# First stage of a two-block fp32 kernel: x's norm by pairs of tiles while x lands, the condition's weights by pairs, and the first four fills interleaved

## The chip, the core and the metric

The kernel runs on one NeuronCore of a Trainium2 chip. The metric is the device time of one execution in microseconds; lower is better. The core has five engines that run their own instruction streams and meet only at semaphores: TensorE (PE, matrix products), VectorE (DVE), ScalarE (ACT), GpSimd (POOL) and SyncE (SP), which here only issues DMAs.

## What is computed

The reference is two transformer-like blocks over x (512 positions by 1,024 channels), all in float32. The change touches only the first lines of the first block:

```python
cond = jax.nn.silu(c.astype(jnp.float32))
mod = cond @ w_ada[l] + b_ada[l]
sh1, sc1, g1, sh2, sc2, g2 = [m[:, None, :] for m in jnp.split(mod, 6, axis=-1)]
u = _layer_norm(h) * (1.0 + sc1) + sh1          # h = x
z = u @ w_in[l]                                 # then HGRN2, gMLP, gates, projections
...
h = _layer_norm(DEEPNORM_ALPHA * h + g1 * mix) * ln1_w[l] + ln1_b[l]
u2 = _layer_norm(h) * (1.0 + sc2) + sh2         # then the FFN, and a second block
```

`_layer_norm` subtracts the mean over the 1,024 channels and divides by the root of the variance. c is one vector of 1,024, w_ada is 1,024 by 6,144.

## The kernel before

x lies transposed in SBUF as `H`: eight tiles (`DT`) of 128 channels by `T` = 512 positions. `bank(b)` is one of the eight PSUM banks, 128 by 512 floats; `A(kb, n, at)` is a stretch of the work area `arena`, and `C("ones", n)` a matrix of ones, so that a product with it sums over the partitions and leaves the sum in every row.

**Fills.** A weight matrix comes in fills: a fill holds the weights of 128 output channels for all eight input tiles (512 KB). SP loads fill n into place n mod 2 of `w_raw`; ScalarE rounds it to fp32r as `w_hi` (`first_hi` L1215, later `hi`), place n mod 4; POOL subtracts and leaves the rest as `w_lo` (`lo_part` L370, four instructions, semaphore `lo_ready`). The same is done to the normed input: `XH` is rounded by ScalarE (`first_x` L1236), `XL` is the remainder from VectorE (`low` L1764). `blocks` (L405) then issues three products of 128x128 by 128x512 for each input tile, `w_hi` with `XH`, `w_lo` with `XH` and `w_hi` with `XL`: 24 products a fill. The last of a fill raises `fill_done`. Only then may ScalarE take the output (`take_hgrn` L1254) and write fill n+4 into the same place of `w_hi`; SP may load over a place of `w_raw` when the fill in it has been split (`lo_ready`).

**The first stage in order.** SP issues x by pairs of tiles (four DMAs), fills 0 and 1, the four parts of w_ada's first 2,048 columns (16 KB a partition each; parts 0 and 1 hold the shift `sh1`, 2 and 3 the scale `sc1`), and then a fill whenever `lo_ready` allows; before fill 4 it also waits for `ada_done` to be 4 and issues four later chunks of w_ada. TensorE sums x (L553, eight products), waits for the squares and sums them (`squares_sum` L524, eight), and in between multiplies the condition with w_ada (`condition_rows` L562: eight products into 32 rows each, four column groups of the array) and turns the result into columns (`condition_columns` L569, four products of one column). Between them stand `idle_products` (L495), products of ones that nobody reads. VectorE centres x (`centred` L1753), multiplies by the root (L1895), adds the bias to the modulation (L1898), and from parts 2 and 3 on scales and shifts tile by tile (L1906). ScalarE squares (L1181), copies the rows out of PSUM (`rows_out` L1229) and computes the root as exp(-0.5 ln v) (`rstd` L1142, L1144). Then fills 0 and 1 go tile by tile in turn, as the tiles become ready, and fills 2 and 3 whole:

```python
first_two(0, 0, 0, lambda t: pe.wait_ge(sem("ln_x"), t + 1))
next_two(0, 0, 0)
gemm(4, 1, 20)
```

After 24 fills TensorE waits for `ada_done` to be 36: VectorE has by then multiplied the later chunks of w_ada with the condition (L1918, L1921). From there on the program is the same in both kernels but for the numbers that semaphores are waited for.

## Time and profile before

| | |
|---|---|
| median of 3 runs | 2936.79 us (2935.02 to 2938.13) |
| the profiled execution's own time | 2937.75 us |
| its span in the profile | 2936.0 us |
| TensorE busy | 2904.3 us, 99% |
| VectorE, ScalarE, POOL busy | 1295.5, 1112.1, 1476.9 us |
| mean granted TensorE clock | 0.998 of full speed |

The page says at a glance which engine has no room: TensorE. Averages say little about the first 63 us, which are 2% of the span, so that stage is read from the timeline (one engine, in order of time), from windows and from the landing times of DMAs. A product's busy time runs over into the next one's (ends are modelled), so the distance of two starts is what one costs.

### The profile page before, as it was taken

The page shows a single profiled execution, that of the slowest core. Times are in us where ns is not written, and L with a number is a line of the kernel's source. Part 1 is how long each engine was busy: PE and PEld are TensorE (multiplying, and loading weights), DVE is VectorE, ACT ScalarE, POOL GpSimd, SP SyncE. Part 2 cuts the span into 40 slices and gives each one's busy share as a digit, 9 for nine tenths or more (in the row PEclk, how much of TensorE's full clock was granted, in tenths as well). Part 3 has the DMA queues.
Part 4 walks back from the last instruction along what each step waited for, and adds up shares of the span by engine and source line. Part 5 has one row for each costly group of instructions (what it writes and reads, how often), then busy time and mean ns, then how long its engine had stood idle before and what let it go on. Part 6 is the DMA issues. An engine that isn't in the chain of part 4 may idle for free.

```text
span 2936.0 us, 52696 instructions
## 1 busy us (share of the span) xinstructions
PE 2904.3 (99%) x20922; PEld 2333.3 (79%) x20922; DVE 1295.5 (44%) x1818; ACT 1112.1 (38%) x1610; POOL 1476.9 (50%) x1824
## 2 busy tenths in 40 slices
PE   9999999999999999999999999999999999999999
PEld 5887778778888777777778888887777777888887
DVE  5837742381110658443757222225944375722210
ACT  4445653243222443225554322224322556432222
POOL 4543345545555556224337555665623343755555
PEclk9999999999999999999999999999999999999999
DMA  6731122213323233225343323333322633423233
GB/s 264 280 103 51 51 94 93 93 58 101 99 96 104 79 122 119 74 79 209 115 158 117 99 93 100 100 107 105 132 71 78 217 111 136 141 94 99 93 102 127
DMA packets 104764, 335.25 MB, mean 114 GB/s; under 512 B 10608, under 2 KB 11024, under 8 KB 103824
## 3 DMA queue, kind: packets, MB, share of 16 engines
q1 hardware_dynamic: 77648, 277.06, 28.5%
q10 hardware_dynamic: 26944, 55.67, 5.1%
q8 instruction: 135, 2.21, 0.3%
q14 instruction: 37, 0.30, 0.0%
HBM read 303.84 MB, written 28.84 MB: 113 GB/s over the span
## 4 chain that ended last, share of the span: by engine, by line
issue 45%; POOL 39%; PE 14%; DVE 1%; POOLq 1%; DMA 0%; ACT 0%; DVEq 0%; SPq 0%; ACTq 0%
POOL w_lo L376 39%; PE psum L405 14%; PE psum L553 0%; POOLq L372 0%; DVE HL L1743 0%; POOLq L382 0%; DVE arena L1753 0%; DVE arena L2379 0%; DMA w_raw<-in_fills 0%; DVEq L1740 0%; PE psum L495 0%; ACT w_hi L1110 0%; DMA par<-in_par 0%; ACT arena L1181 0%; ACT w_hi L1217 0%
## 5 line engine op out<-in xcount | busy, mean ns | idle before, releaser
L376 POOL TENSOR_TENSOR w_lo<-w_raw,w_hi 128x256 fp32r<-128x256 f32 x1820 | 1476.7, 843 | 1454.3 <-ACT w_hi L1110 1306.1
L405 PE MATMUL psum<-XH,w_hi 128*128 128x512 f32 x2592 | 1043.9, 403 | 10.7 <-DVE arena L1989 3.5
L405 PE MATMUL psum<-XL,w_hi 128*128 128x512 f32 x2592 | 1012.3, 391 | 0.0
L405 PE MATMUL psum<-XH,w_lo 128*128 128x512 f32 x2592 | 1012.1, 390 | 0.0
L1110 ACT ACTIVATE w_hi<-w_raw 128x1024 fp32r<-128x1024 f32 x436 | 460.3, 1056 | 689.8 <-PE psum L405 565.0
L405 PEld LDWEIGHTS psum<-XH,w_hi 128*128 128x128 f32 x2592 | 487.3, 188 | 137.0 <-issue 21.1
L405 PEld LDWEIGHTS psum<-XL,w_hi 128*128 128x128 f32 x2592 | 487.6, 188 | 104.3
L405 PEld LDWEIGHTS psum<-XH,w_lo 128*128 128x128 f32 x2592 | 488.1, 188 | 98.5 <-issue 4.8
L405 PE MATMUL psum<-HH,w_hi 128*128 128x512 f32 x976 | 382.0, 391 | 2.5 <-DVE HL L1743 1.5
L405 PE MATMUL psum<-HL,w_hi 128*128 128x512 f32 x976 | 379.9, 389 | 0.0
L405 PE MATMUL psum<-HH,w_lo 128*128 128x512 f32 x976 | 379.8, 389 | 0.0
L405 PEld LDWEIGHTS psum<-HH,w_hi 128*128 128x128 f32 x976 | 183.3, 188 | 42.9 <-DVE HL L1743 3.0
L405 PEld LDWEIGHTS psum<-HL,w_hi 128*128 128x128 f32 x976 | 183.2, 188 | 38.4
L405 PEld LDWEIGHTS psum<-HH,w_lo 128*128 128x128 f32 x976 | 183.3, 188 | 37.4 <-issue 0.2
L805 PEld LDWEIGHTS psum<-arena 64*64 64x64 f32 x6848 | 132.2, 134 | 41.5 <-issue 31.7
L805 PE MATMUL psum<-arena 64*64 64x64 f32 (+1 forms) x6848 | 147.0, 223 | 2.4 <-ACT arena L1580 1.5
L1743 DVE TENSOR_TENSOR HL<-arena,HH 128x512 f32 (+2 forms) x114 | 96.9, 859 | 111.1 <-ACT HH L1212 40.6
L1212 ACT ACTIVATE HH<-arena 128x512 f32 x44 | 27.9, 633 | 189.5 <-DVE arena L1852 189.5
L1535 ACT ACTIVATE arena<-psum 128x512 f32<-128x512 f32 x88 | 52.2, 593 | 107.7 <-PE psum L405 107.3
L1847 DVE TENSOR_TENSOR arena<-psum,arena 128x512 f32<-128x512 f32 x44 | 30.4, 692 | 140.1 <-PE psum L405 120.6
L1776 DVE TENSOR_TENSOR arena<-psum,arena 128x512 f32<-128x512 f32 x22 | 15.2, 691 | 171.9 <-PE psum L405 171.9
L1852 DVE TENSOR_TENSOR arena<-psum,arena 128x512 f32<-128x512 f32 x44 | 30.4, 692 | 116.0 <-PE psum L405 115.4
(341 smaller groups left out, 2368.3 us busy)
## 6 DMA issues: line engine op xcount, KB each, us to landing
w_raw<-in_fills SPq DMA_DIRECT2D x456, 512.0 KB, 3.4
scratch<-arena ACTq DMA_DIRECT2D x86, 256.0 KB, 2.1
arena<-in_fills SPq DMA_DIRECT2D x32, 512.0 KB, 4.5
arena<-scratch ACTq DMA_DIRECT2D x10, 1024.0 KB, 7.5
arena<-in_w_ada SPq DMA_DIRECT2D x4, 2048.0 KB, 19.0
H<-scratch ACTq DMA_DIRECT2D x4, 2048.0 KB, 11.4
scratch<-H SPq DMA_DIRECT2D x2, 2048.0 KB, 8.0
arena<-scratch SPq DMA_DIRECT2D x32, 128.0 KB, 3.8
```

The lines of the kernel that those rows point to most:

```text
L376: ins = nc.gpsimd.tensor_tensor(w_lo[:, to:to + FILL // 4], w_raw[:, of:of + FILL // 4], w_hi[:, to:to + FILL // 4].bitcast(F32), ALU.subt ...
L405: ins = mm(out_ap, wt[:, w:w + 128], xt[:, x0:x0 + T], start=first and k == 0 and o == 0, stop=last and k == n - 1 and o == 2)
L805: ins = mm(bank(b, n, at)[to:to + 64], left[r], right[r], start=first, stop=last)
L1110: fn(w_hi[:, s * FILL:(s + 1) * FILL], w_raw[:, (s % 2) * FILL:(s % 2 + 1) * FILL], ACT.Copy).then_inc(hi_ready, 1)
L1212: fn(HH[:, bass.ds((2 * i + j // 2) * T, T)], A(105, T, j // 2 * T), ACT.Copy).then_inc(sem("ffn_hi"), 1)
L1535: fn(buffer, bank(b), ACT.Sigmoid if GATE_B <= k < RG_AT else ACT.Copy).then_inc(chunk_out[b], 1)
L1743: return tt(dst, src, hi_part.bitcast(F32), ALU.subtract)
L1776: tt(A(105, T, k * T), bank(j), A(88, T, k * T), ALU.mult).then_inc(chunk_out[j], 1)
L1847: tt(A(88, T, k * T), bank(j - 1), A(R_KB), ALU.mult).then_inc(chunk_out[j - 1], 1)
L1852: tt(A(105, T, k * T), bank(j), A(88, T, k * T), ALU.mult).then_inc(chunk_out[j], 1)
```

## The change

- SP: w_ada comes in four pieces by pairs of tiles: piece k holds the shift and the scale of tiles 2k and 2k+1, in two DMAs of 8 KB a partition. The order is x, piece 0, fills 0 and 1, piece 1; then a wait for `lo_ready` 1, fill 2, piece 2; a wait for `lo_ready` 2, fill 3, piece 3. The later chunks of w_ada stand before fill 6 instead of fill 4.
- Norm: the first two tiles of x give a shift (their mean over 256 channels). VectorE adds it to each pair as it has landed, ScalarE squares, and TensorE sums both by pairs into column groups of 32; a total over the groups gives mean and variance. ScalarE squares the mean.
- VectorE subtracts the mean in place (L1962), multiplies by scale and root at once (`scaled`), ScalarE adds the shift as the activation's bias while rounding, and VectorE adds it again for the remainder (`first_low`).
- TensorE: the first four fills go by pairs of tiles, with the condition's products among them; the idle groups of products from L495 behind the second go.

```diff
@@ -285,10 +287,25 @@
             for q in range(4):
                 part = slice(2 * q * T, (2 * q + 2) * T)
                 sp.dma_start(H[:, part], dram["x"][:, part]).then_inc(x_in[q], 16)
+            def ada_piece(k):
+
+                for half in range(2):
+                    of = dram["w_ada"][2 * half + k // 2][:, k % 2 * 8 * KB:(k % 2 + 1) * 8 * KB]
+                    sp.dma_start(A(40 + 16 * k + 8 * half, 8 * KB), of).then_inc(sem(f"ada_in{k}"), 16)
+
+            def first_fill(f):
+
+                sp.dma_start(w_raw[:, f % 2 * FILL:(f % 2 + 1) * FILL], dram["fills"][f]).then_inc(w_loaded[f % 2], 16)
+
+            ada_piece(0)
             for f in range(2):
-                sp.dma_start(w_raw[:, f * FILL:(f + 1) * FILL], dram["fills"][f]).then_inc(w_loaded[f], 16)
-            for k in range(4):
-                sp.dma_start(A(40 + 16 * k, 16 * KB), dram["w_ada"][k]).then_inc(sem(f"ada_in{k}"), 16)
+                first_fill(f)
+            ada_piece(1)
+            for f in range(2, 4):
+                sp.wait_ge(lo_ready, f - 1)
+                first_fill(f)
+                ada_piece(f)
+
...
-            for n in range(2, FILLS_HG + 4 * HEADS // 2 + 2):
+            for n in range(4, FILLS_HG + 4 * HEADS // 2 + 2):
                 a = 2 * (n - 6 - ADA_FILL) + 4
-                if n == 4:
+                if n == 6:
                     sp.wait_ge(sem("ada_done"), 4)
                     for k in range(4):
                         ada_chunk(k)
-            def squares_sum(n):
-
-                for t in range(DT):
-                    if t % 2 == 0:
-                        pe.wait_ge(sem("ln_sq"), 4 * n + t // 2 + 1)
-                    ins = mm(bank(5), C("ones", 128), A(16, T, t * T), start=t == 0, stop=t == DT - 1)
-                ins.then_inc(sem("ln_var"), 1)
+            def group_pair(b, q, tile):
+
+                for t in (2 * q, 2 * q + 1):
+                    g = 32 * (t % 4)
+                    ins = mm(bank(b)[g:g + 32], C("ones", 32), tile(t), start=t < 4, stop=t >= 4)
+                return ins
+
+            def total(b, n):
+
+                pe.wait_ge(sem("ln_groups"), n)
+                return mm(bank(b), C("ones", 128), A(GROUPS_KB), start=True, stop=True)
...
             idle_products(3, 3)
-            for t in range(DT):
-                if t % 2 == 0:
-                    pe.wait_ge(x_in[t // 2], 16)
-                ins = mm(bank(4), C("ones", 128), H[:, t * T:(t + 1) * T], start=t == 0, stop=t == DT - 1)
+            pe.wait_ge(x_in[0], 16)
+            for t in range(2):
+                ins = mm(bank(0), C("ones", 128), H[:, t * T:(t + 1) * T], start=t == 0, stop=t == 1)
             ins.then_inc(sem("ln_sum"), 1)
+            idle_products(2, 3)
+
+            def shifted_pair(q):
+
+                pe.wait_ge(sem("ln_xc"), q + 1)
+                return group_pair(1, q, lambda t: A(0, T, t * T))
+
+            def squared_pair(q):
+
+                pe.wait_ge(sem("ln_sq"), q + 1)
+                return group_pair(3, q, lambda t: A(16, T, t * T))
+
+            shifted_pair(0)
+            for q in range(1, 4):
+                ins = shifted_pair(q)
+                if q == 3:
+                    ins.then_inc(sem("ln_sum"), 1)
+                squared_pair(q - 1)
+            squared_pair(3).then_inc(sem("ln_sum"), 1)
+            total(2, 1).then_inc(sem("ln_sum"), 1)
 
             def condition_rows(k):
 
-                pe.wait_ge(sem(f"ada_in{k}"), 16)
+                pe.wait_ge(sem(f"ada_in{k}"), 32)
                 w = A(40 + 16 * k, 16 * KB).rearrange("p (t k c) -> p t k c", k=DT, c=128)
...
                 for t in range(4):
-                    ins = mm(bank(k, 1, t), A(ROW_KB, 128, k % 2 * T + 128 * t), C("ones", 1), start=True, stop=True)
+                    ins = mm(bank(4 + k % 2, 1, t), A(ROW_KB, 128, k % 2 * T + 128 * t), C("ones", 1), start=True, stop=True)
                 ins.then_inc(sem("ada_used"), 1)
 
             pe.wait_ge(sem("cond"), 2)
-            idle_products(2, 3)
             condition_rows(0)
-            squares_sum(0)
+            total(0, 2).then_inc(sem("ln_var"), 1)
+            condition_columns(0)
             condition_rows(1)
-            condition_columns(0)
+
+            def first_part(f, k):
+
+                if k == 0:
+                    pe.wait_ge(lo_ready, f + 1)
+                pe.wait_ge(sem("ln_x"), k + 1)
+                ins = blocks(f, XH, XL, bank(f), [k], [k], k == 0, k == DT - 1)
+                if k == DT - 1:
+                    ins.then_inc(fill_done, 1)
+
+            def first_pair(f, q):
+
+                for k in (2 * q, 2 * q + 1):
+                    first_part(f, k)
+
+            first_pair(0, 0)
+            condition_columns(1)
+            first_pair(1, 0)
             condition_rows(2)
-            condition_columns(1)
-            idle_products(2, 4)
+            first_pair(0, 1)
+            first_pair(1, 1)
+            condition_columns(2)
+            for q in range(3):
+                first_pair(2, q)
+            first_pair(0, 2)
+            first_pair(1, 2)
             condition_rows(3)
-            condition_columns(2)
-            idle_products(1, 4)
+            first_pair(3, 0)
+            first_pair(3, 1)
             condition_columns(3)
-            idle_products(3, 4)
-            first_two(0, 0, 0, lambda t: pe.wait_ge(sem("ln_x"), t + 1))
-            next_two(0, 0, 0)
+            first_pair(3, 2)
+            for f in range(4):
+                first_pair(f, 3)
             gemm(4, 1, 20)
             pe.wait_ge(sem("ada_done"), 4 + ADA_LATER)
...
+            act.wait_ge(sem("ln_sum"), 4)
+            fn(A(FIRST_SQ_KB), bank(2), ACT.Square, scale=1.0 / 32 / D).then_inc(sem("ln_sq"), 1)
             rows_out(0)
-            for f in range(2):
-                first_hi(f)
-            ln_rstd(0, RSTD_KB)
+            first_hi(0)
+            ln_rstd(0, RSTD_KB, 0, 1.0 / 32 / D)
+            first_hi(1)
 
             def first_x(t):
 
                 act.wait_ge(sem("ln_u"), t + 1)
-                fn(XH[:, t * T:(t + 1) * T], A(16, T, t * T), ACT.Copy).then_inc(sem("ln_hi"), 1)
-
-            for k in range(1, 4):
-                rows_out(k)
-            for t in range(DT):
-                first_x(t)
-                if t == 1:
-                    first_hi(2)
-            first_hi(3)
+                fn(XH[:, t * T:(t + 1) * T], A(16, T, t * T), ACT.Identity, bias=mod[:, t:t + 1]).then_inc(sem("ln_hi"), 1)
+
+            for k in range(4):
+                if k:
+                    rows_out(k)
+                    if k < 3:
+                        first_hi(1 + k)
+                for t in (2 * k, 2 * k + 1):
+                    first_x(t)
...
-            def centred(n, mean):
-
-                dve.wait_ge(sem("ln_sum"), mean)
-                for q in range(4):
-                    stt(chunks(A(0, 2 * T, 2 * q * T), T), bc(bank(4), 2), -1.0 / D, chunks(Ht(2 * q, 2), T), ALU.mult, ALU.add)\
-                        .then_inc(sem("ln_xc"), 1)
-            centred(0, 1)
-            dve.wait_ge(sem("ln_rstd"), 1)
+            dve.wait_ge(sem("ln_sum"), 1)
+            ts(A(FIRST_SHIFT_KB), bank(0), -1.0 / (2 * P), None, ALU.mult)
+            drain()
             for q in range(4):
+                dve.wait_ge(x_in[q], 16)
+                tt(chunks(A(0, 2 * T, 2 * q * T), T), chunks(Ht(2 * q, 2), T), bc(A(FIRST_SHIFT_KB), 2), ALU.add).then_inc(sem("ln_xc"), 1)
+            dve.wait_ge(sem("ln_sum"), 2)
+            cp(A(GROUPS_KB), bank(1)).then_inc(sem("ln_groups"), 1)
+            dve.wait_ge(sem("ln_sq"), 5)
+            stt(A(GROUPS_KB), A(FIRST_SQ_KB), -D / 4.0, bank(3), ALU.mult, ALU.add).then_inc(sem("ln_groups"), 1)
+
+            def centred(q):
+
                 x = chunks(A(0, 2 * T, 2 * q * T), T)
-                tt(x, x, bc(A(RSTD_KB), 2), ALU.mult)
+                stt(x, bc(bank(2), 2), -1.0 / 32 / D, x, ALU.mult, ALU.add)
+
+            def shift_scale(ap):
+
+                return ap.rearrange("p (a n) -> p a n", a=2)
+
+            def modulation(k):
+
+                dve.wait_ge(sem("ada_used"), k + 2)
+                tt(shift_scale(mod[:, 0:16])[:, :, 2 * k:2 * k + 2], shift_scale(bank(4 + k % 2, 4)),
+                   shift_scale(P1("b_ada", 0, 16))[:, :, 2 * k:2 * k + 2], ALU.add)
+                drain()
+                ts(mod[:, 8 + 2 * k:10 + 2 * k], mod[:, 8 + 2 * k:10 + 2 * k], 1.0, None, ALU.add)
+                drain()
+
+            def scaled(t):
+
+                stt(A(16, T, t * T), A(0, T, t * T), mod[:, 8 + t:9 + t], A(RSTD_KB), ALU.mult, ALU.mult).then_inc(sem("ln_u"), 1)
+
+            def first_low(t):
+
+                dve.wait_ge(sem("ln_hi"), t + 1)
+                s = slice(t * T, (t + 1) * T)
+                stt(XL[:, s], A(16, T, t * T), mod[:, t:t + 1], XH[:, s].bitcast(F32), ALU.add, ALU.subtract).then_inc(sem("ln_x"), 1)
+
+            centred(0)
+            centred(1)
             for k in range(4):
-                dve.wait_ge(sem("ada_used"), k + 2)
-                tt(mod[:, 4 * k:4 * k + 4], bank(k, 4), P1("b_ada", 4 * k, 4), ALU.add)
+                modulation(k)
+                if k == 0:
+                    dve.wait_ge(sem("ln_rstd"), 1)
+                for t in (2 * k, 2 * k + 1):
+                    scaled(t)
                 if k < 2:
-                    continue
-                drain()
-                ts(mod[:, 4 * k:4 * k + 4], mod[:, 4 * k:4 * k + 4], 1.0, None, ALU.add)
-                drain()
-                t0 = 4 * (k - 2)
-                for t in range(t0, t0 + 4):
-                    ts(A(16, T, t * T), A(0, T, t * T), mod[:, 8 + t:9 + t], mod[:, t:t + 1], ALU.mult, ALU.add).then_inc(sem("ln_u"), 1)
-                    if t > t0:
-                        low(0, t - 1)
-                low(0, t0 + 3)
```

How the orders of three engines change. SP, at the start of the program (`in_w_ada` are the condition's weights), before:

```order
L287 DMA H<-in_x 128x1024 x4
L289 DMA w_raw<-in_fills 128x1024 x2
L291 DMA arena<-in_w_ada 128x4096 x4
L315 DMA w_raw<-in_fills 128x1024 [waits lo_ready] x2
L299 DMA arena<-in_fills 128x1024 [waits ada_done]
L299 DMA arena<-in_fills 128x1024 x3
L315 DMA w_raw<-in_fills 128x1024 [waits lo_ready] x6
```

and now:

```order
L289 DMA H<-in_x 128x1024 x4
L294 DMA arena<-in_w_ada 128x2048 x2
L298 DMA w_raw<-in_fills 128x1024 x2
L294 DMA arena<-in_w_ada 128x2048 x2
L298 DMA w_raw<-in_fills 128x1024 [waits lo_ready]
L294 DMA arena<-in_w_ada 128x2048 x2
L298 DMA w_raw<-in_fills 128x1024 [waits lo_ready]
L294 DMA arena<-in_w_ada 128x2048 x2
L332 DMA w_raw<-in_fills 128x1024 [waits lo_ready] x2
L316 DMA arena<-in_fills 128x1024 [waits ada_done]
```

Pieces 2 and 3 of the condition's weights now stand behind a wait for the split of fills 0 and 1.

TensorE, from the second wait for the condition's weights on (L562 and L602 are rows, L569 and L609 columns), before:

```order
L562 MATMUL psum<-arena 32x512 [waits ada_in1]
L562 MATMUL psum<-arena 32x512 x7
L569 MATMUL psum<-con,arena 128x1 [waits ada_row]
L569 MATMUL psum<-con,arena 128x1 x3
L562 MATMUL psum<-arena 32x512 [waits ada_in2]
```

and now, to the first product of the second fill's first pair:

```order
L602 MATMUL psum<-arena 32x512 [waits ada_in1]
L602 MATMUL psum<-arena 32x512 x7
L422 MATMUL psum<-XH,w_hi 128x512 [waits ln_x,lo_ready]
L422 MATMUL psum<-XH,w_lo 128x512
L422 MATMUL psum<-XL,w_hi 128x512
L422 MATMUL psum<-XH,w_hi 128x512 [waits ln_x]
L422 MATMUL psum<-XH,w_lo 128x512
L422 MATMUL psum<-XL,w_hi 128x512
L609 MATMUL psum<-con,arena 128x1 [waits ada_row]
L609 MATMUL psum<-con,arena 128x1 x3
L422 MATMUL psum<-XH,w_hi 128x512 [waits ln_x,lo_ready]
```

The first products of fill 0 come between the rows of piece 1 and their columns; before, all rows and columns came first.

ScalarE, from the first copy of rows on, before:

```order
L1229 ACTIVATE arena<-psum 128x512 [waits ada_done]
L1217 ACTIVATE w_hi<-w_raw 128x1024 [waits w_loaded0]
L1217 ACTIVATE w_hi<-w_raw 128x1024 [waits w_loaded1]
L1142 ACTIVATE arena<-psum,con 128x512 [waits ln_var]
L1144 ACTIVATE arena<-arena 128x512
L1229 ACTIVATE arena<-psum 128x512 [waits ada_done] x3
```

and now:

```order
L1294 ACTIVATE arena<-psum 128x512 [waits ln_sum]
L1291 ACTIVATE arena<-psum 128x512 [waits ada_done]
L1279 ACTIVATE w_hi<-w_raw 128x1024 [waits w_loaded0]
L1204 ACTIVATE arena<-psum,con 128x512 [waits ln_var]
L1206 ACTIVATE arena<-arena 128x512
L1279 ACTIVATE w_hi<-w_raw 128x1024 [waits w_loaded1]
L1303 ACTIVATE XH<-arena,mod 128x512 [waits ln_u] x2
L1291 ACTIVATE arena<-psum 128x512 [waits ada_done]
L1279 ACTIVATE w_hi<-w_raw 128x1024 [waits w_loaded0]
```

Fill 1 is split behind the root, and the split of fill 0 stands behind the squared mean.

## Rows read from the trace of the kernel before

**Rows 1.** The page, section 1: busy us, share of the span and instructions of each engine.

```profile
PE 2904.3 (99%) x20922; PEld 2333.3 (79%) x20922; DVE 1295.5 (44%) x1818; ACT 1112.1 (38%) x1610; POOL 1476.9 (50%) x1824
```

**Rows 2.** Windows: length, busy us of each engine, clock, DMA share, GB/s.

```profile
0.00:40.00 40.00, 34.40 (x154) 17.38 (x155) 14.54 (x33) 15.98 (x20) 5.74 (x12) 1.00 0.87 345
...
62.70:171.50 108.80, 108.80 (x482) 89.98 (x480) 73.47 (x115) 44.91 (x50) 67.99 (x84) 1.00 0.66 237
```

**Rows 3.** Timeline, TensorE: start us, us, engine, line, op, count, [idle before <-releaser].

```profile
6.91 8.76 PE L553 MATMUL psum<-H,con 128*128 128x512 f32 x16
...
10.36 0.19 PEld L553 LDWEIGHTS psum<-H,con 128*128 128x128 f32 x1 [0.42 <-issue]
...
17.94 1.92 PE L562 MATMUL psum<-arena 128*32 128x512 f32 x16 [1.40 <-DMA arena<-in_w_ada]
...
28.71 1.05 PE L569 MATMUL psum<-con,arena 128*128 128x1 f32 x8
...
34.01 1.92 PE L562 MATMUL psum<-arena 128*32 128x512 f32 x16 [0.44 <-DMA arena<-in_w_ada]
...
39.63 0.47 PE L405 MATMUL psum<-XH,w_hi 128*128 128x512 f32 x1
...
46.31 0.50 PE L405 MATMUL psum<-XH,w_hi 128*128 128x512 f32 x1 [0.75 <-DVE XL L1743]
...
62.78 0.39 PE L405 MATMUL psum<-XH,w_hi 128*128 128x512 f32 x1
```

**Rows 4.** DMAs: the condition's issue, its landings, and the page's fills.

```profile
5.47 1.99 SPq L291 DMA_DIRECT2D arena<-in_w_ada  x4
...
DMA to landing us min/median/max: 12.4/19.0/27.0
...
w_raw<-in_fills SPq DMA_DIRECT2D x456, 512.0 KB, 3.4
```

**Rows 5.** Timeline, VectorE, columns as in rows 3.

```profile
15.71 4.62 DVE L1753 SCALAR_TENSOR_TENSOR arena<-psum,H 128x1024 f32<-128x1024 f32 x4 [7.69 <-PE psum L553]
...
38.68 0.69 DVE L1743 TENSOR_TENSOR XL<-arena,XH 128x512 fp32r<-128x512 f32 x1 [0.24 <-ACT XH L1239]
...
41.24 2.38 DVE L1743 TENSOR_TENSOR XL<-arena,XH 128x512 fp32r<-128x512 f32 x2
...
43.76 0.47 DVE L1902 TENSOR_SCALAR mod<-mod 128x4 f32<-128x4 f32 x1
...
151.01 5.17 DVE L1921 SCALAR_TENSOR_TENSOR arena<-arena,cond 128x256 f32<-128x256 f32 x7
```

**Rows 6.** Timeline, ScalarE, columns as in rows 3.

```profile
16.97 4.45 ACT L1181 ACTIVATE arena<-arena 128x1024 f32<-128x1024 f32 x4 [10.19 <-DVE arena L1753]
...
39.07 1.04 ACT L1217 ACTIVATE w_hi<-w_raw 128x1024 fp32r<-128x1024 f32 x1
...
51.47 1.28 ACT L1254 ACT_TABLE_LOAD   x1 [2.09 <-PE psum L405]
52.76 0.60 ACT L1254 ACTIVATE arena<-psum 128x512 f32<-128x512 f32 x1
53.26 1.06 ACT L1110 ACTIVATE w_hi<-w_raw 128x1024 fp32r<-128x1024 f32 x1
```

**Rows 7.** Timeline, POOL: splits with VectorE quiet, and beside it.

```profile
22.93 5.53 POOL L376 TENSOR_TENSOR w_lo<-w_raw,w_hi 128x256 fp32r<-128x256 f32 x8 [22.48 <-ACT w_hi L1217]
...
40.19 4.02 POOL L376 TENSOR_TENSOR w_lo<-w_raw,w_hi 128x256 fp32r<-128x256 f32 x4 [11.73 <-ACT w_hi L1217]
```

**Rows 8.** Timeline, TensorE, two later stretches with long starts' distances.

```profile
326.89 0.50 PE L405 MATMUL psum<-XH,w_hi 128*128 128x512 f32 x1 [1.75 <-DVE arena L1989]
...
331.08 0.41 PE L405 MATMUL psum<-XL,w_hi 128*128 128x512 f32 x1
...
414.09 0.80 PE L405 MATMUL psum<-XH,w_hi 128*128 128x512 f32 x1 [3.26 <-POOL w_lo L376]
...
419.80 0.43 PE L405 MATMUL psum<-XL,w_hi 128*128 128x512 f32 x1
```

46 lines of the change are left out of this document (25 added, 21 removed).

## The prediction, made before the change was timed

> **What bounds the kernel now.** I read the page first: TensorE is busy in 2904.3 of 2936.0 us [rows 1], so the kernel can only gain in the 32 us where it is not, or where it does work that is not needed. The windows show where: of the first 40 us it is busy in 34.4, and from 62.70 to 171.50 in all 108.8 [rows 2]. So what the first stage saves or loses stands in the time of the kernel in full, provided that later work is not late. The timeline of the first 63 us gives the stage. The statistics of x run from 6.91 to 15.51; the condition's weights land piece by piece until the last rows product starts at 34.01; the fills begin at 39.63, break off until 46.31, and run without a break from there: fill 4 begins at 62.78 [rows 3]. From 46.31 to 62.78 there are 72 products, so one takes 0.229 us. **62.78 is the number to compare**: after it both kernels do the same products.
>
> **What happens to TensorE's work.** The sums over x and over its squares were 16 float products at 0.86 us each. Now two such products give the shift, sixteen products into 32 rows give the sums, and two totals follow. All of this ends before the fills can start, and three idle groups go too; none of it is the gain. The gain is meant to come from the 96 products of fills 0 to 3 (22 us) starting at 27 instead of 39.6 us. Against it stand two new waits of SP, so I follow the chain.
>
> **Until fill 0 is split.** Step by step, in us:
> - The first 16 passes over x start at 6.91; from 10.36 on they are 0.43 apart, and 12 of them fill 10.36 to 15.51, so the first four took 0.86 each: the clock is half (1.2 GHz) until 10.3 [rows 3]. The two products of the shift are just these four passes. VectorE gets them at 10.55 (15.51 to 15.71 was the same handover).
> - Shift 0.7, then four additions of 1,024 columns at 1.16 (4.62 for four [rows 5]): 15.9. The products over x never waited in the trace, so its last tiles were there by 13.8, before the fourth addition starts: only VectorE paces this. The last square is done 1.15 later (4.45 for four [rows 6]): 17.1. A pair of products 0.86: 18.0. The total 0.86: 18.9.
> - Rows of piece 0: 1.86 (1.92 with the tail [rows 3]), landed by 17.9: 20.8. ScalarE copies them (0.60), then splits fill 0 (1.04 [rows 6]): 22.5. Two steps of ScalarE for the root, 23.9, two scalings, 25.2, a centring of two tiles, 26.3, and the remainder of tile 0, 27.0, are what fill 0's first product waits for. POOL takes 2.8 for a fill with VectorE quiet and 4.0 beside it [rows 7]; here VectorE is busy, partly with inputs from PSUM. I take 3.4: **fill 0 is split at 26.0**. Bounds 25.3 and 26.6.
>
> **The queue that now waits.** Before, SP issued all four condition DMAs at 5.47 [rows 4] and the engines never ran dry until 34. Now fill 2 and, behind it, piece 2 wait for 26.0, and fill 3 with piece 3 for fill 1's split, 29.4. The traced pieces landed 12.4 after their issue at the earliest, 19.0 in the middle and 27.0 at the latest [rows 4]; with issues some 0.5 apart that is 17.9, 22.8, 27.7 and 33.9, so a piece of 2,048 KB takes 4.9. Everything ahead of the new waits (x, two fills, two pieces) is the same bytes and has landed by 22.8. So the DMA engines stand for some 5 us: issue 26.0, fill 2 lands 3.4 later [rows 4], piece 2 at **34.3**, and piece 3 at 40.4 instead of 33.9. TensorE has meanwhile done rows 1 (22.8 to 24.7), fill 0's first pair (from 27.1), the columns of piece 1 (1.0 [rows 3]) and fill 1's first pair, until 31.0, and stands for 3.3.
>
> **From piece 2 to fill 4.** 34.3; rows 2, 36.2; twelve products, 38.9; columns 2, 39.9; twelve, 42.7; six whose operands come from VectorE (modulation 0.5, two scalings and two remainders at 0.6 [rows 5]: 43.0 for the second), 44.1; twelve, 46.8; rows 3, 48.7 (piece 3 landed at 40.4: hidden by 6 us); twelve, 51.4; columns 3, 52.4. Now TensorE waits in part: modulation 53.0, remainder of tile 6 at 54.8, of tile 7 at 55.4. Fill 0 ends at 56.4, the other three at 60.5. But fill 4 needs the place of fill 0: ScalarE loads its table (1.28), takes the output (0.60) and splits (1.06) [rows 6], POOL 3.4: 56.6 + 2.9 + 3.4 + 0.1 = **63.0**. Before, fill 0 ended 11 us ahead of fill 4 and this chain of 6.3 was hidden; now it is cover that is gone, and a wait of 2.5. The end is 63.0 against 62.8: **+0.2** before the clock is counted.
>
> **The clock.** TensorE is at 2.4 GHz all through the first stage from 10.3 on, with idle stretches up to 1.40 [rows 3]. After 1.75 idle at 326.89 ten products took 0.43 each, about 2.0 lost; after 3.26 at 414.09 the half clock lasted until 419.8, about 3 lost [rows 8]. The change makes two such stretches. Between 24.7 and 34.3 TensorE has only 4 us of work; if the clock falls there, that work doubles and fills the gap by itself, so the fall costs between 0.2 and 3: I take 1. Before fill 4 the 2.5 costs 0 to 2: I take 1. **Sum +2.2.**
>
> Edits at nothing: the 8 KB pieces carry the same bytes; the renumbered semaphores change no order; the condition's later chunks (now behind fills 4 and 5) start 6 us later on VectorE, and their last sum ended at 156.2 [rows 5], and TensorE asks for it only after 171.5 [rows 2], so 15 us cover that. The scalings and remainders have an operand more but the same columns.
>
> **A rule against this change.** Two remainders took 2.38 while POOL worked and 0.69 when it did not [rows 5, 7]. The Trainium skill ("SBUF — State Buffer", Who interferes with whom) says that a VectorE instruction with two SBUF inputs and a GpSimd instruction that reads SBUF exclude each other for the whole instruction. By the rule fill 0's split would take some 4.2, since the two scalings fall into it, and tile 4's chain would lose another 0.7: the sum would be about +3.7 instead of +2.2. The trace's pair agrees with it.
>
> **How this stands to the runs.** The sum against the profiled execution's own 2937.75 is 2940.0; that execution lies 0.96 above the median of 2936.79, so against the median it is **2939.0**.
>
> **Rivals.**
> - *The queue is not late.* For it: every split without contention, the clock up throughout. Fill 0's split at 25.3, fill 4 0.6 shorter: 63.0 - 0.7 - 0.6 = 61.7, that is -1.1, and -3 if the handovers are also shorter: 2934 to 2936. Against it: the 2.38 and the idle stretches.
> - *Products into 32 rows don't run side by side in twos.* Decisive place: TensorE between 12.4 and the total. The trace's eight products into 32 rows take 1.92, that is four at a time [rows 3]. Sixteen products one by one take 13.8 from 12.5 on and end at 26.3 instead of 18.0, and the whole chain is 8 later: 2947, slower. It turns slower from 3.7 more than forecast. A pair lies in two different column groups, which speaks against it.
> - *Contention and clock together.* VectorE and POOL hold each other up in both chains (+3) and the half clock is in force from 34.3 for 5.8 us and again at fill 4 (+3 more): 2942 to 2945.
> - *More is won than any row shows.* To gain 5.9, fill 4 would have to start at 56.9; with rows 1 done at 24.7, the 96 products, two groups of rows and two of columns alone end at 52.5 if they wait for nothing, and fill 0 would have to end by 50.5. Only another place could give it, such as the later clock falls at 327 and 414, which cost 5 together.
> - *The change doesn't do what it says*: fills 0 and 1 don't begin before 34 because fill 1's split or the norm is late. That leaves twelve products to be caught up, 2.7 more: within the forecast's upper range.
>
> **How the numbers follow.** A measurement of this kernel tells about 0.2% (5.9 us) from no change. Forecast with its bounds (2936 to 2942): 0.55. Queue not late: 0.18. Early products late: 0.05. Contention and clock: 0.09, half of it above 2942.7. Serial pairs: 0.08. More won, or later clock falls gone: 0.05, nearly all counted as faster. So faster 0.07, same 0.78, slower 0.15 (with 0.02 for what I don't see). The range leaves out the outer cases, 2933 to 2944.5.
>
> **What would show it.** In the profile after: fill 2's DMA issue near 26 and no DMA traffic from 23 to 28; rows 2 starting near 34; the last first-fill product near 60.5, and a wait of TensorE for w_lo before fill 4 at 63 to 65; half clock near 27 to 34. Wrong if piece 2 lands before 32, if fill 4 starts before 61, or if the column-group products take over 1.2 us a pair. If fill 4's start moves and the total doesn't, the place after it is not covered as [rows 2] says.

## The result, and the profile after

The changed kernel takes **2945.6 us** (median of 8 runs, 2943.73 to 2948.98) against 2936.24 (8 runs, 2935.02 to 2938.13) on the same chip: ratio 1.0030, 95% interval 1.0021 to 1.0039. It is slower by 9.4 us (0.3%), more than the 0.2% that can be told from no change, and above the range given (2933 to 2944.5). Its profiled execution took 2943.73 us, span 2941.9; that of before took 2937.75, span 2936.0. So the two profiles show 6.0 us of the 9.4: before's lies 1.5 above the median of 2936.24, the changed kernel's is the fastest of its 8. The mean granted clock is 0.997 (0.998 before).

The page says that TensorE does less and still ends later [rows 1]:

```profile
PE 2899.5 (99%) x20918; PEld 2326.9 (79%) x20918; DVE 1297.7 (44%) x1823; ACT 1114.4 (38%) x1611; POOL 1475.8 (50%) x1824
```

Windows, columns as in rows 2:

```profile
0.00:40.00 40.00, 28.76 (x136) 12.63 (x137) 22.35 (x39) 18.77 (x23) 11.40 (x17) 0.91 0.84 330
...
68.00:72.00 4.00, 4.00 (x12) 3.17 (x11) 3.52 (x5) 1.41 (x2) 3.25 (x5) 0.57 0.37 134
70.00:180.00 110.00, 110.00 (x490) 89.64 (x488) 71.90 (x115) 47.94 (x54) 69.49 (x87) 0.99 0.68 239
```

From 70 to 180 TensorE is as full as it was from 62.7 on, so nothing there makes good what the first stage loses. The stage itself, TensorE's timeline (L573 the two products of the shift, L512 idle products, L540 the sums of x by pairs, L602 the condition's rows, L609 its columns, L422 the fills' products):

```profile
7.10 1.98 PE L573 MATMUL psum<-H,con 128*128 128x512 f32 x4
8.92 1.03 PE L512 MATMUL psum<-con 128*128 128x256 f32 x4
11.16 5.54 PE L540 MATMUL psum<-arena,con 128*32 128x512 f32 x32 [1.22 <-DVE arena L1953]
...
23.28 2.90 PE L602 MATMUL psum<-arena 128*32 128x512 f32 x16 [1.82 <-DMA arena<-in_w_ada]
26.40 0.77 PE L422 MATMUL psum<-XH,w_hi 128*128 128x512 f32 x1 [0.22 <-DVE XL L1985]
...
34.81 3.35 PE L602 MATMUL psum<-arena 128*32 128x512 f32 x16 [3.99 <-DMA arena<-in_w_ada]
38.09 0.50 PE L422 MATMUL psum<-XH,w_hi 128*128 128x512 f32 x1
...
40.99 0.95 PE L609 MATMUL psum<-con,arena 128*128 128x1 f32 x8
...
45.11 0.50 PE L422 MATMUL psum<-XH,w_hi 128*128 128x512 f32 x1 [0.29 <-DVE XL L1985]
...
58.01 0.50 PE L422 MATMUL psum<-XH,w_hi 128*128 128x512 f32 x1 [1.38 <-DVE XL L1985]
...
67.62 0.49 PE L422 MATMUL psum<-XH,w_hi 128*128 128x512 f32 x1 [3.87 <-POOL w_lo L393]
```

The fills do begin at 26.40 and not at 39.63 [rows 3]. Rows 2 wait 3.99 for their piece and then run at half clock (3.35; 1.92 for the same rows before). Rows 3 follow at 49.42, columns 3 at 54.17, the first product of pair 3 at 58.01, and fill 4 at **67.62**: 4.84 later than 62.78. SyncE's queue (L298 a fill, L294 half a piece each) shows where piece 2 was; the DMA share of the first 60 us, in 40 slices of 1.5 us, shows the hole that it left:

```profile
25.05 0.33 SPq L298 DMA_DIRECT2D w_raw<-in_fills  x1
25.42 0.91 SPq L294 DMA_DIRECT2D arena<-in_w_ada  x2
28.70 0.33 SPq L298 DMA_DIRECT2D w_raw<-in_fills  x1
```

```profile
DMA  0488999999999950069999999980082000199997
```

The end of the stage, ScalarE and then POOL:

```profile
56.45 1.38 ACT L1303 ACTIVATE XH<-arena,mod 128x512 fp32r<-128x512 f32 x2 [4.43 <-DVE arena L1979]
57.11 0.40 ACTq L1313 DMA_DIRECT2D con<-in_con  x1
57.54 0.51 ACTq L1314 DMA_DIRECT2D par<-in_par  x1
59.75 1.28 ACT L1318 ACT_TABLE_LOAD   x1 [1.92 <-PE psum L422]
62.67 0.60 ACT L1318 ACTIVATE arena<-psum 128x512 f32<-128x512 f32 x1 [1.64 <-DMA par<-in_par]
63.17 1.05 ACT L1172 ACTIVATE w_hi<-w_raw 128x1024 fp32r<-128x1024 f32 x1
...
64.29 5.81 POOL L393 TENSOR_TENSOR w_lo<-w_raw,w_hi 128x256 fp32r<-128x256 f32 x7 [21.63 <-ACT w_hi L1172]
```

Ahead of fill 0's output ScalarE waits for the constants and parameters that its own queue fetches. In both kernels the two DMAs are issued behind tile 7. Before, ScalarE went from its table straight to the output [rows 6]; its rows and the landing times of the stretch from 40 to 70 us say by how little:

```profile
48.25 0.44 ACTq L1250 DMA_DIRECT2D par<-in_par  x1
```

```profile
par<-in_par ACTq DMA_DIRECT2D x1, 68.0 KB, 4.4
```

Issued at 48.25 and landed 4.4 later, they were there at 52.65, 0.1 before ScalarE's 52.76. Now they are issued at 57.54, ScalarE is ready 3.49 later (61.03), and they land 5.1 after the issue.

From fill 4 the loss grows to 6.5 us at the later condition sums (they start at 171.7 before, 178.2 now), most of it in the half clock of 68.00 to 72.00 above, and is 5.9 at the end.

### The profile page after: what moved, and what is told of

Its sections match the earlier page's. It is cut to its first block, busy times and chain, and to the rows that moved or that the text cites. A ratio compares the mean times of both kernels' runs of the same rounds, so it can differ in the third digit from the quotient of the medians.

```text
span 2941.9 us, 52706 instructions
## 1 busy us (share of the span) xinstructions
PE 2899.5 (99%) x20918; PEld 2326.9 (79%) x20918; DVE 1297.7 (44%) x1823; ACT 1114.4 (38%) x1611; POOL 1475.8 (50%) x1824
## 4 chain that ended last, share of the span: by engine, by line
PE 47%; issue 25%; POOL 21%; DVE 4%; DVEq 1%; DMA 1%; ACT 1%; POOLq 0%; ACTq 0%; SPq 0%
PE psum L422 40%; POOL w_lo L393 21%; PE psum L867 3%; DVEq L1804 1%; DMA arena<-scratch 1%; PE psum L1120 0%; PE psum L553 0%; PE psum L1100 0%; DVE arena L2536 0%; DVE HL L1807 0%; PE psum L1136 0%; DMA w_raw<-in_fills 0%; DVE arena L2526 0%; PE psum L1143 0%; PE psum L1141 0%
## 5 line engine op out<-in xcount | busy, mean ns | idle before, releaser
L422 PE MATMUL psum<-XH,w_hi 128*128 128x512 f32 x2592 | 1045.0, 403 | 15.7 <-POOL w_lo L393 7.1
L422 PE MATMUL psum<-XL,w_hi 128*128 128x512 f32 x2592 | 1012.8, 391 | 0.0
L422 PE MATMUL psum<-XH,w_lo 128*128 128x512 f32 x2592 | 1012.8, 391 | 0.0
L422 PEld LDWEIGHTS psum<-XH,w_hi 128*128 128x128 f32 x2592 | 487.7, 188 | 146.9 <-issue 29.2
L422 PEld LDWEIGHTS psum<-XL,w_hi 128*128 128x128 f32 x2592 | 487.9, 188 | 104.5
L422 PEld LDWEIGHTS psum<-XH,w_lo 128*128 128x128 f32 x2592 | 488.3, 188 | 98.3 <-issue 4.8
L422 PE MATMUL psum<-HH,w_hi 128*128 128x512 f32 x976 | 382.0, 391 | 2.2 <-DVE HL L1807 1.3
L422 PE MATMUL psum<-HL,w_hi 128*128 128x512 f32 x976 | 379.9, 389 | 0.0
L422 PE MATMUL psum<-HH,w_lo 128*128 128x512 f32 x976 | 379.8, 389 | 0.0
L422 PEld LDWEIGHTS psum<-HH,w_hi 128*128 128x128 f32 x976 | 183.2, 188 | 42.6 <-DVE HL L1807 2.7
L422 PEld LDWEIGHTS psum<-HL,w_hi 128*128 128x128 f32 x976 | 183.2, 188 | 38.4
L422 PEld LDWEIGHTS psum<-HH,w_lo 128*128 128x128 f32 x976 | 183.3, 188 | 37.6 <-issue 0.2
```

Source lines behind the costliest of these rows:

```text
L422: ins = mm(out_ap, wt[:, w:w + 128], xt[:, x0:x0 + T], start=first and k == 0 and o == 0, stop=last and k == n - 1 and o == 2)
```

## The experiments

Each ratio is to the kernel before on the same chip, with its 95% interval. "Fill 4" is the start of its first product in the profiled execution, "from the sums" its distance from the first product of the sums by pairs (11.16 in the changed kernel).

| run | median us | ratio | fill 4 | from the sums |
|---|---|---|---|---|
| changed kernel | 2945.60 | 1.0030 (1.0021 to 1.0039) | 67.62 | 56.46 |
| the same again | 2945.10 | 1.0027 (1.0017 to 1.0037) | 67.67 | 56.61 |
| piece 2 early | 2940.96 | 1.0015 (1.0006 to 1.0024) | 62.96 | 51.53 |
| constants early | 2943.14 | 1.0019 (1.0010 to 1.0028) | 67.17 | 54.76 |
| both | 2938.06 | 1.0006 (0.9997 to 1.0015) | 64.39 | 52.55 |
| all pieces early, order kept | 2942.52 | 1.0019 (1.0010 to 1.0028) | 68.05 | 55.96 |
| idle products ahead of fill 4 | 2947.52 | 1.0034 (1.0022 to 1.0046) | 68.88 | 56.22 |
| idle products ahead of rows 2 | 2948.62 | 1.0046 (1.0032 to 1.0059) | 68.41 | 56.79 |
| norm by pairs alone | 2940.07 | 1.0004 (0.9994 to 1.0013) | 64.81 | 53.79 |
| the same with idle products | 2938.01 | 0.9999 (0.9990 to 1.0008) | 61.80 | 50.47 |
| early pairs | 2934.94 | 0.9990 (0.9981 to 0.9999) | 58.22 | 46.69 |
| early pairs with idle products | 2936.81 | 1.0001 (0.9992 to 1.0010) | 59.02 | 46.74 |
| early pairs again | 2934.56 | 0.9993 (0.9984 to 1.0002) | 59.15 | 46.70 |

The last column is needed because the sums don't begin at the same time in every execution. The four passes that give the shift took 1.82 us in the changed kernel's (7.10 to 8.92 above), but 3.22 in the run with the constants early and 3.46 in the run with idle products ahead of fill 4, where their pace was half as fast to begin with. With the constants early:

```profile
6.95 3.38 PE L573 MATMUL psum<-H,con 128*128 128x512 f32 x4
10.17 1.03 PE L512 MATMUL psum<-con 128*128 128x256 f32 x4
12.41 5.55 PE L540 MATMUL psum<-arena,con 128*32 128x512 f32 x32 [1.22 <-DVE arena L1954]
```

(The clock column of the windows reads 1.00 over this stretch in all of them; only the distances of starts show it.) The edits come later in the program, so this part of a shift is chance. It carries through to POOL's first split, which began 10.14 to 10.15 after the sums in the six executions of the table's first six rows.

### The changed kernel again

> The changed kernel once more, for a second profile of it and for its median on the chip that runs the kernels beside it. Theory A (its loss is structural: fill 4 starts about 5 us later, and on top of that TensorE's clock falls once or more where it idles in the first stage, at places that differ by execution): median 2943 to 2947 us; fill 4 starts at 67 to 69 us; pair 3 starts at 57.5 to 59.5 us after a wait on VectorE's XL; the wait of ScalarE ahead of its fold of the weights' scale on the parameters' DMA is again 1.3 to 2 us. Theory B (the profiled execution was an odd one): fill 4 at 62 to 65 us and a median within 3 us of the kernel before.

Theory A: the loss is in the kernel and not in one execution. Pair 3 starts at 58.06 and fill 4 at 67.67, and the parameters' wait is 1.57. What differs is the clock: rows 1 took 1.92 at full clock this time, and the half clock lay at 27.7 to 38.2 (granted clock 0.51), in the end of the first products, the columns and rows 2.

```profile
22.88 1.92 PE L602 MATMUL psum<-arena 128*32 128x512 f32 x16 [1.53 <-DMA arena<-in_w_ada]
...
28.50 1.70 PE L609 MATMUL psum<-con,arena 128*128 128x1 f32 x8
```

### Piece 2 ahead of the wait

```diff
             ada_piece(1)
+            ada_piece(2)
             for f in range(2, 4):
                 sp.wait_ge(lo_ready, f - 1)
                 first_fill(f)
-                ada_piece(f)
+            ada_piece(3)
```

> The changed kernel with one DMA pair moved: piece 2 of the condition's weights is issued right behind piece 1, ahead of the wait for fill 0's split; piece 3 stays behind both waits. Theory A (the new waits in SP's queue cost the time): piece 2 lands near 27.7 instead of 34.8, so its rows products start near 31, right behind fill 1's first pair, and at full clock (1.9 us instead of 3.35). Fill 4 then starts some 5 us earlier than 67.6, near 62.5, and the median is near 2940.5. Theory B (the time is lost only in the chain that fill 4 needs after fill 0's end, whatever is in front): the stage is as long as before, fill 4 near 67, 2945 to 2946. Theory C (clock alone): less than 2 us gained, 2944.

```profile
30.89 1.93 PE L603 MATMUL psum<-arena 128*32 128x512 f32 x16
...
53.34 0.50 PE L423 MATMUL psum<-XH,w_hi 128*128 128x512 f32 x1 [1.37 <-DVE XL L1986]
...
62.96 0.79 PE L423 MATMUL psum<-XH,w_hi 128*128 128x512 f32 x1 [3.89 <-POOL w_lo L394]
```

(The edit shifts line numbers by one.) Rows 2 start 3.9 earlier, with no wait and at full clock; fill 4 starts 4.7 earlier (4.9 from the sums). ScalarE's split of fill 2, which stands ahead of tiles 2 and 3, now waits 3.72 for its fill (1.55 before the edit), and TensorE waits 0.48 behind rows 2. Piece 2 behind the new wait is the largest part of the loss: by the ratios 0.12 to 0.15%, some 4 us. The median came where Theory A had it.

### Constants and parameters issued after tiles 4 and 5

```diff
                 for t in (2 * k, 2 * k + 1):
                     first_x(t)
+                if k == 2:
+                    tail = CONST["cd"]
+                    act.dma_start(con[:, 256:tail], dram["con"][:, 256:tail]).then_inc(sem("const_in"), 16)
+                    act.dma_start(par2[:], dram["par2"]).then_inc(sem("const_in"), 16)
...
-            tail = CONST["cd"]
-            act.dma_start(con[:, 256:tail], dram["con"][:, 256:tail]).then_inc(sem("const_in"), 16)
-            act.dma_start(par2[:], dram["par2"]).then_inc(sem("const_in"), 16)
```

> The changed kernel with ScalarE's two DMAs of later constants issued after the rounding of tiles 4 and 5 instead of after tile 7 (57.1 us). In the changed kernel ScalarE waits 1.64 us for them before it takes fill 0's output. Theory A: that wait is part of the chain to fill 4, so fill 4 starts 1.6 us earlier, near 66.0, and the median is near 2944. Theory B (POOL or the clock hides it): no change, 2945.6, and the 1.6 us show up as a wait elsewhere on ScalarE. If the two DMAs delay piece 3 or fill 5, the columns of piece 3 come later than 54.2; I don't expect that, since the DMA engines are quiet from 41 to 51.

```profile
59.03 0.51 PE L422 MATMUL psum<-XH,w_hi 128*128 128x512 f32 x1 [1.37 <-DVE XL L1986]
...
67.17 0.49 PE L422 MATMUL psum<-XH,w_hi 128*128 128x512 f32 x1 [2.38 <-POOL w_lo L393]
```

From pair 3 to fill 4 it is 8.14 instead of 9.61, which is the 1.5 of the wait. In this execution pair 3 itself came 1.0 later, because the sums had begun 1.25 later, so that fill 4 is only 0.45 earlier; from the sums it is 1.7 earlier. The ratio is below the changed kernel's, but the intervals overlap: by itself this run shows the wait gone, not a shorter time.

### Both

> Condition piece 2 issued ahead of SyncE's wait for fill 0's split, and the constants' and parameters' DMAs on ScalarE's queue issued after tiles 4 and 5 rather than after tile 7. Theory A (the two causes are separate and add up: 4.6 us by the first and 1.5 us by the second of the shift of fill 4): fill 4 starts at 61 to 62.5 us, that is at or before the 62.78 of the kernel before, and the median is 2937.5 to 2940.5 us, equal to the kernel before to within 0.1%. Theory B (both reach the same wait, so that they overlap): fill 4 at 62.9 to 63.5 us and 2940 to 2942 us.

```profile
56.26 0.50 PE L423 MATMUL psum<-XH,w_hi 128*128 128x512 f32 x1 [1.37 <-DVE XL L1987]
...
64.39 0.49 PE L423 MATMUL psum<-XH,w_hi 128*128 128x512 f32 x1 [2.38 <-POOL w_lo L394]
```

The medians add up: ratio 1.0006, which cannot be told from no change, where the changed kernel beside it gave 1.0027, and the two intervals don't touch. So these two places explain nearly all of the loss. Fill 4 missed the number (64.39), because the half clock lay in this execution at 28 to 35, on products and the start of rows 2; from pair 3 (56.26) the chain is again 8.13.

### Idle products ahead of fill 4

An idle product is two passes of 256 columns, so 8 of them are 16 instructions.

```diff
                 first_pair(f, 3)
+            idle_products(8)
             gemm(4, 1, 20)
```

> The changed kernel with eight products of ones (128x256, 0.43 us each, 3.4 in all) between the last product of the first four fills and fill 4, where TensorE stands for 3.87 us. They compute nothing that is used. Theory A (the clock falls because of that idle time): fill 4 starts at the same 67.6, the granted clock stays at 1.0 behind it, eight products that took 0.43 us take 0.23, and the median is 1.7 us lower, near 2943.9. Theory B (the clock falls for another reason, or the products themselves hold fill 4 up): 2945.6 or more.

```profile
64.84 3.61 PE L512 MATMUL psum<-con 128*128 128x256 f32 x16
68.88 0.49 PE L422 MATMUL psum<-XH,w_hi 128*128 128x512 f32 x1 [0.43 <-POOL w_lo L393]
```

The half clock behind fill 4 is gone, and with it 1.6 us: from fill 4 to the later condition sums it took 109.0 rather than 110.6. Fill 4 itself was not held up: from pair 3 (59.25) it is 9.63, as in the changed kernel (9.61); it is late because the sums began 1.5 later. So Theory A holds as far as the sums at 178, and the whole was not faster all the same. In this execution TensorE waited 2.9 at 1409 for VectorE's residual H, which it did not in the changed kernel.

### Idle products ahead of rows 2

```diff
             first_pair(1, 0)
+            idle_products(8, 3)
             condition_rows(2)
```

> The changed kernel with 8 idle products (256 columns each) in TensorE's wait for condition piece 2. Theory A (the half clock in rows 2 comes from that empty wait, 1.4 us of the time): rows 2 at 34.8 us but in 1.9 us rather than 3.35, pair 3's start 1.3 to 1.6 us earlier (56.4 to 56.9), fill 4 at 66.0 to 66.6; median 1 to 2 us below the changed kernel's, 2943 to 2944.5. Theory B (the clock had fallen before the wait, at the short stretches between 23 and 28 us, or falls in what is left of the wait): rows 2 at 3.3 us or more again and the median as the changed kernel's, 2945 us.

```profile
32.94 4.92 PE L512 MATMUL psum<-con 128*128 128x256 f32 x16
37.79 1.92 PE L602 MATMUL psum<-arena 128*32 128x512 f32 x16
```

Both theories fall. The clock was low from 28.70 on, so the 8 idle products began in it and took 4.92; rows 2 got the full clock and 3.0 us of delay. Here filling the wait cost more than the clock it brought back: pair 3 started at 59.54, 1.5 later than in the changed kernel.

### The norm by pairs alone

All pieces issued at once, all rows and columns ahead of the fills, fills 0 and 1 in turn, then 2 and 3 whole, fills 2 and 3 split after tiles 5 and 7: nearly the order of before (which splits fill 2 after tile 1), with the new norm.

```diff
-            first_pair(0, 0)
             condition_columns(1)
...
+            for k in range(DT):
+                for j in range(2):
+                    first_part(j, k)
+            for j in range(2, 4):
+                for k in range(DT):
+                    first_part(j, k)
```

> The norm by shifted tiles, the pieces by pairs and the root joined to the modulation stay; undone are SP's waits inside the pieces (all four pieces at once, then fills 2 and 3 behind their waits) and the interleaving: all rows and columns first, fills 0 and 1 tile by tile in turn, fills 2 and 3 whole, fill 2 and 3 split after the tiles. Theory A (waits in the queue and the new order lose the time, the norm gains): the last piece lands near 33, its columns end near 37, all eight tiles are ready by 40, fills 0 and 1 run without a break, fill 4 starts near 60.5 instead of 62.8 in the kernel before, median near 2934. Theory B (the norm is what loses): fill 4 later than 64 and the median above 2938.

```profile
24.00:44.60 20.60, 17.99 (x76) 9.19 (x69) 13.30 (x23) 7.94 (x12) 7.30 (x9) 0.50 0.59 242
```

By its numbers (fill 4 at 64.81, median 2940.07) this is Theory B, but the norm is not what the trace shows as the cause. It shows the clock: after 1.99 idle ahead of rows 1, TensorE ran at 1.2 GHz for over 20 us, through all rows, columns and the first fill products. The idle groups that the change takes out stood there.

### The same with idle products in the gaps

```diff
             condition_columns(0)
+            idle_products(8, 3)
             condition_rows(1)
+            idle_products(3, 3)
...
             condition_columns(1)
+            idle_products(3, 3)
             condition_rows(2)
+            idle_products(3, 3)
             condition_columns(2)
             condition_rows(3)
+            idle_products(3, 3)
             condition_columns(3)
```

> The run with the norm alone once more, with idle products in the gaps between rows and columns (8 after columns 0, 3 after rows 1, 3 after columns 1, 3 after rows 2, 3 after rows 3), as the kernel before has them. Theory A (TensorE's clock fell there because the change leaves those gaps empty, and thin rows and columns did not bring it up): granted clock 1.0 from rows 1 on, rows 2 and 3 in 1.9 us each, the first fill product at 38 to 39.5 us against 41.44, fill 4 at 59.5 to 61 us; 2934 to 2937.5 us. Theory B (the clock falls all the same, or the gaps are too long to be covered): rows 2 at 3.4 to 3.7 us again and 2938 to 2942 us.

```profile
24.00:39.90 15.90, 15.14 (x102) 9.09 (x100) 10.91 (x17) 6.34 (x10) 6.15 (x8) 1.00 0.68 281
```

```profile
61.80 0.39 PE L422 MATMUL psum<-XH,w_hi 128*128 128x512 f32 x1
```

Theory A on the clock: 1.00 all through, rows 2 and 3 in 1.92 each. Fill 4 starts at 61.80, 3.0 before that of the run without idle products and 1.0 before the 62.78 of before; the first fill product (39.94), fill 4 and the median are each a little above what Theory A gave. The median cannot be told from before, so no gain of the norm by pairs, by itself, shows. (This execution has the wait of 2.2 for H that is told of under what stays open.)

### All pieces early, the change's order kept

```diff
-            ada_piece(1)
+            for k in range(1, 4):
+                ada_piece(k)
             for f in range(2, 4):
                 sp.wait_ge(lo_ready, f - 1)
                 first_fill(f)
-                ada_piece(f)
```

and the constants as above.

> The changed kernel's own order of TensorE and ScalarE (first four fills pair by pair), with all condition pieces issued at once on SyncE and the constants' and parameters' DMAs after tiles 4 and 5: only the order then parts it from the early-pairs version, whose fill 4 started at 58.22 us. Theory A (SyncE's queue behind the fills' wait and the two late DMAs were the loss; the order itself costs only the short chain from pair 3 to fill 4, about 8 us from pair 3's first product by the runs e1 and e2, which whole fills hide): rows 2 at about 31 us, pair 3 starts at 49 to 52 us, fill 4 at 58.5 to 61 us behind a wait on GpSimd of 1 to 3.5 us; median 2935.5 to 2938.5 us. Theory B (ScalarE's split of fill 2, which stands ahead of x tiles 2 and 3 in this order, waits for a fill that now lands behind three pieces, and holds up the x tiles): pair 3 starts later than 53 us, fill 4 later than 61.5 us; 2939 us or more.

```profile
35.44 1.06 ACT L1279 ACTIVATE w_hi<-w_raw 128x1024 fp32r<-128x1024 f32 x1 [8.85 <-DMA w_raw<-in_fills]
```

```profile
31.54 1.92 PE L602 MATMUL psum<-arena 128*32 128x512 f32 x16
...
37.95 0.80 PE L422 MATMUL psum<-XH,w_hi 128*128 128x512 f32 x1 [4.49 <-DVE XL L1986]
```

Theory B. Rows 2 are there at 31.54, but ScalarE's split of fill 2 stands ahead of tiles 2 and 3 in this order and waits 8.85 for the fill, which now lands behind three pieces. So issuing every piece first does not mend this order: fill 2 is needed early in it. With piece 2 early and piece 3 left behind ("Both", with the same constants) the wait for fill 2 was 3.78, TensorE had rows 2 without a wait, and the median came back to that of before, not below it.

### Early pairs

The same pieces and constants; ScalarE splits fill 2 after tiles 4 and 5 and fill 3 last; TensorE puts into the gaps only products of fills 0 and 1:

```diff
             first_pair(0, 0)
             condition_columns(1)
             first_pair(1, 0)
             condition_rows(2)
             first_pair(0, 1)
-            first_pair(1, 1)
             condition_columns(2)
-            for q in range(3):
-                first_pair(2, q)
-            first_pair(0, 2)
-            first_pair(1, 2)
             condition_rows(3)
-            first_pair(3, 0)
-            first_pair(3, 1)
+            first_pair(1, 1)
             condition_columns(3)
-            first_pair(3, 2)
-            for f in range(4):
-                first_pair(f, 3)
+            for q in range(2, 4):
+                first_pair(0, q)
+                first_pair(1, q)
+            for j in range(2, 4):
+                for q in range(4):
+                    first_pair(j, q)
```

> A version meant to beat both kernels: the norm by pairs and the four pieces as in the changed kernel, all four pieces issued at once on SyncE, the constants' and parameters' DMAs after tiles 4 and 5, the products of fills 0 and 1 for pairs 0 and 1 put between the rows and columns (where TensorE waited), fills 2 and 3 whole behind them. Theory A (what lost time was idle time of TensorE between 24 and 58 us, and the last fills' split then hides ScalarE's chain to fill 4): fill 4 starts at 56 to 59 us, 4 to 6 us before the 62.78 of the kernel before; 2931 to 2934 us. Theory B (the pieces then delay fills 2 and 3 in their landing, or the clock stays low through the thin rows and columns as in the run with the norm alone): fill 4 at 60 to 63 us and 2936 to 2941 us.

```profile
30.98 1.92 PE L602 MATMUL psum<-arena 128*32 128x512 f32 x16
...
35.72 1.92 PE L602 MATMUL psum<-arena 128*32 128x512 f32 x16
...
44.46 0.50 PE L422 MATMUL psum<-XH,w_hi 128*128 128x512 f32 x1 [0.59 <-DVE XL L1983]
...
58.22 0.39 PE L422 MATMUL psum<-XH,w_hi 128*128 128x512 f32 x1
```

Theory A for the stage: from 44.46 TensorE has no wait, rows 3 start at 35.72 rather than 49.42, and fill 4 starts 4.56 before 62.78 with its chain hidden behind two whole fills. The median (2934.94 against 2937.80) lies between the ranges of the two theories; the profiled execution was the fastest of its 11.

> The early-pairs version once more, for a second interval, since the first (ratio 0.9990, from 0.9981 to 0.9999) only just leaves out no difference. Theory A (its earlier fill 4, by 4.6 us, is a gain that stays to the end): ratio 0.998 to 0.9995 again, 2932 to 2935.5 us, fill 4 at 57.5 to 59 us. Theory B (falls of the clock later give it back): ratio 0.9995 to 1.0005, 2936 to 2938 us, with fill 4 early all the same.

Theory A by ratio and median: 3.5 us below before (2934.56 against 2938.10), though this interval just reaches 1. Fill 4 (59.15) is a little above its range, because the sums began at 12.45 and not at 11.53. Two independent runs put this version 0.07 to 0.1% below before, which is at the edge of what they can tell, and clearly below the changed kernel.

> The early-pairs version (2934.94 us on the chip of the last call, 2930.97 in its profiled execution) with 8 idle products behind columns 0, in the wait for piece 1. Theory A (what lifts its other executions above the profiled one is a fall of the clock in that wait, in some of them): rows 1 at 24.5 to 25.2 us at the full clock, 1.5 to 2.5 us later than without, fill 4 within 1 us of 58.2, median 2932 to 2934.5. Theory B (the spread comes from elsewhere, and the idle products only delay rows 1): fill 4 at 59 to 60, median 2935 to 2937 us.

Theory B by its numbers, but not for its reason. The clock rose a little (0.9984 over its executions, 0.9978 without). Rows 1 started at 26.07 and not 22.67, yet fill 4 is as far from the sums as without idle products (46.74, against 46.69 and 46.70): the delay is gone by rows 2 (31.78, against 30.98), and fill 4 is 0.8 later because the sums began at 12.28. The median was as before's; in the profiled execution TensorE waited 2.92 for H at 1399, after ScalarE had waited long for a fill:

```profile
1382.22 1.06 ACT L1170 ACTIVATE w_hi<-w_raw 128x1024 fp32r<-128x1024 f32 x1 [6.77 <-DMA w_raw<-in_fills]
```

## Why the prediction was wrong

The chain to fill 4 was the right thing to follow and most of its steps hold. Fill 4 was put at 63.0 and came at 67.62. Of these 4.6 us, 0.5 stand ahead of rows 2, 2.6 between rows 2 and pair 3 (1.4 of it half clock), and 1.5 between pair 3 and fill 4. Two steps failed: the chain behind fill 0 was costed at 6.4 with the load that ScalarE's output reads at nothing, and took 7.9; and the clock, allowed 2 in all, took 3.1 in the profiled execution (1.4 in rows 2, 1.7 behind fill 4).

- **Until fill 0 is split.** The order of steps was right, the time partly by luck. The half pace of the first four passes, read from the trace before, was taken over (3.44), and this execution took 1.82 for them, so that VectorE had the shift at 9.12 and not at 10.55. The pairs of products into 32 rows run side by side (5.54 for 32, the last ones paced by ScalarE's squares), so that rival fell. The split ended by 25.05, just outside the bounds of 25.3 and 26.6 (predicted 26.0), begun at 21.31: 3.7, between the 3.4 that I took from the rows and the 4.2 that I drew from the rule of the Trainium skill ("SBUF — State Buffer", Who interferes with whom). VectorE's two scalings beside it took 1.89 against 1.41 later, with POOL quiet. POOL's 0.9 over its quiet 2.8 and VectorE's 0.5 make the 1.4 that two scalings last: the trace agrees with the rule, and my 4.2 had put all of the waiting on POOL.
- **The queue that now waits.** Right in kind, and the time by two misses that cancel: fill 2 was issued at 25.05, 0.95 early, but rows 2 started at 34.81 against 34.3. Fill 2 landed as reckoned (ScalarE had it at 28.37); piece 2 then took 6.4 and not 4.9. Fill 3 was issued at 28.70, while it was on its way; the last piece before, with fills issued behind it, had taken 6.2 by the prediction's own landing times (27.7 to 33.9). No run separates that. The wait it makes, 3.99, is the larger cause of the loss against before; the early issue of piece 2 took it away, and 4.7 us with it.
- **The chain behind fill 0.** "this chain of 6.3 was hidden; now it is cover that is gone" was right, but the list of what the cover had hidden stopped at table, output and splits. It left out the load that ScalarE's output waits for. Fill 0's last six products now follow tile 7 at once, no longer in turn with fill 1's, so the reader came 1.0 closer to the issue, and the DMA took 0.7 longer: a margin of 0.1 became a wait of 1.64. I had costed the chain at 6.4; it took 7.9.
- **From piece 2 to pair 3.** Predicted 34.3 to 54.9, measured 34.81 to 58.01: 23.2 and not 20.6. Rows 2 at half clock are 1.4 of it. The rest is in steps of 0.1 to 0.4: groups after a change of kind start some 0.1 late, and columns 3 to pair 3 took 3.84, not 3.5.
- **The clock, taken as 1 + 1.** Mis-sized: 3.1 in this execution. The gap before fill 4 was not 2.5 but 3.87, and cost 1.7 more behind it. In the first gap the half clock fell on rows, which are on the path, and not only on products that wait anyway. The executions of the changed kernel had a mean granted clock of 0.9964 (9 of them), those of before beside them 0.9983 (31); one thousandth of the time is 2.9 us, so the clock may stand for up to 5.5 of the 7.3 us between their medians. That is an estimate, and part of it is already in the 4.9 by which fill 4 is late.
- **"Contention and clock together" came nearest of the rivals**, by its clock and without its contention: 2942 to 2945 was its range, 0.09 its chance, and 2945.6 lies above even that. The range should have reached over it, since both gaps were in my own sum.
- **The order.** I costed it as work that moves, at a gain offset by the pieces. No run of this order gained: with late pieces TensorE waits for piece 2, with all pieces first it waits 4.49 behind fill 2, and with piece 2 and the constants early it comes back to the time of before. With only fills 0 and 1 brought forward there is a gain of some 0.1%.

What stays open: between 1397 and 1411 TensorE waited 2.2 to 2.9 for H in the profiled executions of all four kernels with added idle products in the first stage, 1.1 in the second of early pairs, 0.6 with piece 2 early, and not at all in the other eight. In all four ScalarE had waited 6.4 to 6.8 for a fill's DMA some 17 us before, against 1.8 to 1.9 in the other ten. Four of four is hardly chance, but how products some 1,300 us earlier come to this no run here tells; it is why their totals are weak evidence on the clock. Nor was it tried how the changed kernel's timed executions differ from the profiled ones, which were the fastest of their kind in both: 3.4 of the 9.4 us are in no profile.
